# A decoder block with 32 streamed experts on one core: order of VectorE's mixing steps, of the router's products and table, of the third expert's first fetch, and of the last bias product

## Chip, core and metric

The kernel runs on one core of one Trainium2 chip, in float32. The time is the device time of the whole kernel in microseconds. Below, PE is TensorE, DVE is VectorE, ACT is ScalarE, POOL is GpSimd and SP is SyncE, whose queue issues nearly all loads.

## What is computed

```python
def reference(x, ...):                 # x: 1 x 256 x 1024, one layer
    u = rms_norm(h, norm1_g)
    proj = u @ w_in                    # 1024 x 4608
    y_conv = conformer_conv(proj[..., :c1], ...)          # ends in @ w_conv_out
    y_attn = moba_attention(q, k, v, ...) @ w_attn_out    # 8 heads of 64
    g = sigmoid(proj[..., c4:] + b_gates)
    mixed = g[..., :D] * y_conv + g[..., D:] * y_attn
    h = h + mixed @ w_out
    u2 = rms_norm(h, norm2_g)
    h = h + moe_ffn(u2, ...)           # 32 experts, the 4 best of each token

def moe_ffn(xf, ...):
    logits = xf @ w_router + b_router
    top_v, top_i = top_k(logits, 4); gates = softmax(top_v)
    # for each expert e, its tokens in rows:
    #   h = x @ w_up_gate[e] + b_up_gate[e]
    #   a = min(h[:, :F], 7); lin = clip(h[:, F:], -7, 7)
    #   y = (a * sigmoid(1.702 a) * (lin + 1)) @ w_down[e] + b_down[e]
    #   out[token] += y * gate
```

There are 256 tokens and 1024 features. An expert has 8 MiB of up and gate weights and 4 MiB of down weights, and every one of the 32 is used.

## The kernel before

The engines run hand-written instruction streams side by side and wait for each other through semaphores; nothing is scheduled by a compiler. On each engine the order is that of the code.

**Mixing stage.** Products of float32 weights are made of three products each: a high part times a high part, and each high part times the other's low part (`product3`, L1084). ACT writes high parts (`weights_high`, L537), DVE the low ones (`weights_low`, L728), in halves `b` of a weight group `i`: `ATT_W` is w_attn_out, `CONV_W` w_conv_out, `OUT_W` and `OUT_W + 1` the halves of w_out. PE makes four banks of attention products (uses `U_ATT + b` of the four shared banks), four banks of conv products (`U_CONV + b`), which go into the same banks, and then the products of w_out, with 512 columns each. Before it writes a bank it claims it: it waits until the last reader of that bank, four uses back, has freed it. DVE multiplies the attention banks with their gates (L862, the mixing products), and for each conv bank it makes a product and a sum (L877 and L881), which complete a quarter of `mixT` (`mix_ready`). ACT copies the quarter as a high part (`mix_hi`), and DVE makes its low part (`mix_low`, L869), for which PE's w_out products wait.

**Router.** PE turns the new h (`transpose_h`), DVE scales it to `u2T`, and `logits(m)` multiplies token tile m with the router's weights (L1061). Four `seed` products (L1275) put h into the four accumulator banks of the output. DVE finds the four best experts of each token; from these come tables in several steps that go back and forth between DVE and PE: positions of tokens (L1294 to L1298), number of tiles of 32 slots per expert (`exp_col[:, 0]`), keys that put experts with many tiles at turns in the order of experts (L1302, L1309), the experts at their turns (L1320 to L1322), ends (L1335), and last the rows that go to the integer table `cum` (L1339 to L1343). `cum` holds the first item of each turn, the expert and tile of each item, and the order of experts; its last write is signalled by `cum_ready` (L1002). Between these steps PE gathers the rows of the first tile (L1286), turns the gates (L1315, copied by ACT to `gates_t`), and makes the bias product of the first tile (`bias`, L1326).

**Experts.** Expert by expert in the order of the table, PE runs `tile` once per 32 slots: up products (L1365, 8 steps k, 32 matmuls that the trace counts as 64), scatter of the tile before (L1349), gather of the next, the bias product of the next tile (L1326), and down products (L1396). Each step's end is signalled: `up_quarter` after k = 1 (first expert only), `up_done[0]` after k = 3, `up_done[1]` after k = 7, `down_done`.

**Weights.** There are two buffers of each kind, even and odd. The parts of experts 0 and 1 are loaded by fixed number while the stages before still run, as their space in the buffers comes free: SP waits for PE's use of the scratch that lies there (`used(sp, i)`, `mix_ready`, `out_half`). Every later expert is fetched by its number, which SP reads from `cum` with a register load (`value_load`): `fetch` waits for `up_done` and `down_done` of the expert two turns earlier. The third expert's up weights go in quarters (`fetch_up_sooner`, L422), the first of them behind `up_quarter`.

## Time and profile before

| | |
|---|---|
| time, median of 3 runs | 1107.93 us (1107.56 to 1110.68) |
| profiled execution | 1109.64 us, its span 1107.9 us |
| granted TensorE clock, mean | 0.908 |
| PE, DVE, ACT busy | 918.5, 448.4, 252.4 us |
| loaded from HBM | 431.59 MB, 391 GB/s over the span |

The span is from the first to the last instruction in the trace. A busy share of an engine is an average over stages that have different limits. The granted clock is the share of full speed that the chip allows PE in a stretch: 1.00 is 2.4 GHz and 0.50 is 1.2 GHz. Times within the span are counted from its start.

### The profile page before, as it was taken

Reading aid. Unit: us, or ns where it says so; the run is one execution under the profiler, and the core shown is the slowest. Engines: PE = TensorE matmul, PEld = TensorE weight load, DVE = VectorE, ACT = ScalarE, POOL = GpSimd, SP = SyncE. Lnnn points to the kernel's source line nnn. Section 1 sums busy time; section 2 is a strip of 40 time slices with the busy share of each in tenths; the row PEclk is TensorE's granted clock in tenths of the full one; section 3 lists DMA queues with packets and bytes.
Section 4 is the critical chain, followed back from the end, with each engine's and each line's share of the span. In section 5 each row is a group of like instructions: output and inputs, shape, how many; then the busy total and the mean of one; then the engine's idle time right before and its main releaser. Section 6 shows DMA issues by size and latency. Waiting matters only on the chain.

```text
span 1107.9 us, 18786 instructions
## 1 busy us (share of the span) xinstructions
PE 918.5 (83%) x7003; PEld 425.0 (38%) x7004; DVE 448.4 (40%) x1106; ACT 252.4 (23%) x404; POOL 6.0 (1%) x29
## 2 busy tenths in 40 slices
PE   7999999998666669789976799986995965997666
PEld 6998888532111123233322233331331321332122
DVE  5899875442222223334432244442441422343222
ACT  4665573221111111212221011121220211122111
POOL 1000000000000000000000000000000000000000
PEclk9999899898788788889998899998997988998878
DMA  7664278999999999999999999999999999999996
GB/s 278 217 245 153 77 289 343 378 434 432 427 431 433 434 433 431 427 433 435 434 429 428 431 435 434 433 427 431 433 435 432 431 427 433 435 434 429 428 430 272
DMA packets 30647, 432.98 MB, mean 391 GB/s; under 512 B 2725, under 2 KB 3137, under 8 KB 16288
## 3 DMA queue, kind: packets, MB, share of 16 engines
q1 hardware_dynamic: 29640, 431.83, 92.1%
q10 hardware_dynamic: 984, 0.82, 0.2%
q8 instruction: 17, 0.28, 0.1%
q14 instruction: 6, 0.05, 0.0%
HBM read 431.59 MB, written 1.05 MB: 391 GB/s over the span
## 4 chain that ended last, share of the span: by engine, by line
PE 59%; DMA 28%; another core or an unknown queue 6%; DVE 4%; ACT 2%; issue 1%; SPq 0%; ACTq 0%; DVEq 0%
PE bank L1365 26%; DMA up_even<-in_w_up_gate 16%; PE bank L1396 10%; PE bank L1084 9%; DMA up_odd<-in_w_up_gate 8%; DMA down_even<-in_w_down 4%; PE bank L1349 3%; PE bank L1326 3%; PE bank L1286 3%; DVE up_odd L759 2%; DMA down_odd<-in_w_in 1%; DVE w_lo L728 1%; PE bank L1061 1%; PE bank L1379 1%
## 5 line engine op out<-in xcount | busy, mean ns | idle before, releaser
L1365 PE MATMUL bank<-up_even,reg_r 128*32 128x512 f32 x1472 | 204.6, 714 | 77.0 <-DMA up_even<-in_w_up_gate 77.0
L1365 PE MATMUL bank<-up_odd,reg_r 128*32 128x512 f32 x1408 | 183.9, 677 | 74.9 <-DMA up_odd<-in_w_up_gate 74.9
L1044 DVE SCALAR_TENSOR_TENSOR ys<-bank,gslot,ys 64x512 fp32r<-64x512 f32 x90 | 67.4, 749 | 228.7 <-ACT ys L683 227.2
L1365 PEld LDWEIGHTS bank<-up_even,reg_r 128*32 128x32 f32 x1472 | 53.4, 128 | 224.1 <-issue 139.2
L683 ACT ACTIVATE ys<-bank,gslot 64x512 fp32r<-64x512 f32 x90 | 61.5, 683 | 315.3 <-PE bank L1396 314.1
L1365 PEld LDWEIGHTS bank<-up_odd,reg_r 128*32 128x32 f32 x1408 | 48.7, 123 | 207.4 <-issue 123.7
L677 ACT ACTIVATE reg_m<-reg_m 128x256 f32<-128x256 f32 x45 | 18.9, 420 | 429.5 <-DVE reg_m L1023 429.5
L1396 PE MATMUL bank<-down_odd,reg_r 128*32 128x512 f32 x704 | 81.8, 606 | 11.1 <-DMA down_odd<-in_w_down 11.1
L1023 DVE TENSOR_SCALAR reg_m<-bank 128x256 f32<-128x256 f32 x45 | 19.1, 425 | 172.8 <-PE bank L1365 172.8
L1396 PE MATMUL bank<-down_even,reg_r 128*32 128x512 f32 x736 | 83.7, 595 | 4.8 <-DMA down_even<-in_w_down 4.8
L677 ACT ACT_TABLE_LOAD x45 | 57.7, 1283 | 6.9 <-issue 6.1
L1349 PE MATMUL bank<-ys,hotT 128*128 128x512 f32 x184 | 55.3, 421 | 1.8 <-DVE ys L1044 1.8
L1084 PE MATMUL bank<-u_hi,w_hi 128*128 128x256 f32 x176 | 52.3, 297 | 0.9 <-issue 0.9
L1326 PE MATMUL bank<-bup,sel 128*128 128x512 f32 x92 | 52.7, 655 | 0.0
L1084 PE MATMUL bank<-u_lo,w_hi 128*128 128x256 f32 x176 | 50.7, 288 | 0.0
L1084 PE MATMUL bank<-u_hi,w_lo 128*128 128x256 f32 x176 | 50.7, 288 | 0.0
L1286 PE MATMUL bank<-reg_h,reg_r 128*32 128x256 f32 x736 | 49.3, 385 | 0.7 <-DVE reg_r L910 0.7
L920 DVE TENSOR_SCALAR sel<-quarter_of,pick 128x128 f32<-128x128 f32 x46 | 13.1, 284 | 88.8 <-PE bank L1365 88.8
L759 DVE SCALAR_TENSOR_TENSOR up_odd<-up_odd,reg_m 128x256 f32<-128x256 f32 x120 | 48.6, 482 | 0.0
L1349 PEld LDWEIGHTS bank<-ys,hotT 128*128 128x128 f32 x184 | 30.9, 188 | 45.8 <-issue 38.6
L910 DVE TENSOR_SCALAR reg_r<-iota,pos,st 128x32 f32 (+1 forms) x92 | 23.3, 298 | 61.2 <-issue 61.2
L1396 PEld LDWEIGHTS bank<-down_odd,reg_r 128*32 128x32 f32 x704 | 21.0, 111 | 69.3 <-issue 49.2
(250 smaller groups left out, 1077.4 us busy)
## 6 DMA issues: line engine op xcount, KB each, us to landing
up_odd<-in_w_up_gate SPq DMA_DIRECT2D x30, 4096.0 KB, 47.1
up_even<-in_w_up_gate SPq DMA_DIRECT2D x28, 4096.0 KB, 39.7
down_even<-in_w_down SPq DMA_DIRECT2D x15, 4096.0 KB, 42.6
down_odd<-in_w_down SPq DMA_DIRECT2D x14, 4096.0 KB, 46.8
up_even<-in_w_up_gate SPq DMA_DIRECT2D x7, 2048.0 KB, 11.9
down_even<-in_w_in SPq DMA_DIRECT2D x6, 2048.0 KB, 8.6
up_odd<-in_w_up_gate SPq DMA_DIRECT2D x4, 2048.0 KB, 11.9
down_odd<-in_w_down SPq DMA_DIRECT2D x8, 1024.0 KB, 32.2
```

Source lines behind the costliest of these rows:

```text
L677: nc.scalar.activation(ACT_B, ACT_A, ACT.Sigmoid, scale=ALPHA).then_inc(sigm_ready, 1)
L683: nc.scalar.activation(ys[0:64, half, :], YB[r, :], ACT.Identity, scale=gslot[r, :]).then_inc(y_high, 1)
L759: ins = nc.vector.scalar_tensor_tensor(cv[:, c, :], tap, dwT[:, c, w:w + 1], cv[:, c, :], ALU.mult, ALU.add)
L910: nc.vector.tensor_scalar(hot[:, m, :], slot, pos[:, m, e], st[:, 6 + m:7 + m], ALU.is_equal, ALU.mult).then_inc(hot_built, 1)
L1023: nc.vector.tensor_scalar(ACT_A, UP[:, 0:256], LIMIT, None, ALU.min).then_inc(clip_ready, 1)
L1044: nc.vector.scalar_tensor_tensor(ys[64:P, half, :], YB[r, :], gslot[0:64, :], ys[0:64, half, :].bitcast(F32), ALU.mult, ALU.subtract).then ...
L1084: ins = mm(o, lhs(a, k), rhs(b, k), start=(k == 0 and i == 0), stop=(k == n - 1 and i == 2))
L1286: ins = mm(o[q * SLOTS:(q + 1) * SLOTS, 0:256], hot[:, m, :], hx[:, m, 256 * q:256 * q + 256], start=(m == 0), stop=(m == MT - 1))
L1326: mm(UP[:], sel[:], bup[:], start=True, stop=False, skip_group_check=True)
L1349: ins = mm(acc[2 * m + half][:], hotT[:, m, :], ys[:, half, :], start=False, stop=False, skip_group_check=True)
L1365: ins = mm(UP[q * SLOTS:(q + 1) * SLOTS, :], XT[:, k, :], up_columns(a, k, q), start=False, stop=(k == KD - 1), skip_group_check=True)
L1396: ins = mm(YB[row:row + SLOTS, :], actT[:, r, :], down[a][:, r, half * 512:(half + 1) * 512], start=(r < 2), stop=(r >= KD - 2), skip_grou ...
```

## The change

It has four parts.

1. In DVE's mixing stage the four mixing products come ahead of the low part of w_conv_out's second half; the low part of w_out's second half goes behind the third sum.
2. In the router the halves of `logits(0)` stand around the second tile's transposes, the fourth seed stands behind the product L1302, the first bias product ahead of the turn products, the product that gives the order with the turn products, and the gate products are cut in two. They have their own bank part (`GT`) and semaphores.
3. DVE writes the number of tiles of the first expert (`T_LEAD`) and the order of experts to `cum` as soon as it has them, with a semaphore for each. SP reads the third expert's number behind these, and waits for `cum_ready` only behind its fetch.
4. In the tile of the last expert the next bias product goes behind the down products.

```diff
         UP, ROWS, GA, YB = bank[0:4]
+        GT = ROWS[2 * E:4 * E, T:2 * T]
         def up_columns(a, k, q):
...
             load_down(1, 0, 1)
-            sp.wait_ge(cum_ready, 1)
             def expert_of(t):
...
                 down(a, e, items)
-            fetch(2, 0, fetch_down, fetch_up_sooner)
+            sp.wait_ge(lead_ready, 1)
+            lead = sp.value_load(cum[0:1, T_LEAD:T_LEAD + 1], min_val=1, max_val=ITEMS - 1)
+            sp.wait_ge(order_ready, 1)
+            third = expert_of(2)
+            fetch_up_sooner(0, third, lead)
+            fetch_down(0, third, lead)
+            sp.wait_ge(cum_ready, 1)
             fetch(3, 1, fetch_down)
...
             ins.then_inc(expg, 1)
-            full(act, U_GT)
-            nc.scalar.activation(gT[:], bank[U_GT % 4][0:2 * E, 0:T], ACT.Identity).then_inc(bank_free[U_GT % 4], 1)
+            act.wait_ge(gt_full, 1)
+            nc.scalar.activation(gT[:], GT, ACT.Identity).then_inc(gt_copied, 1)
             act.wait_ge(cum_ready, 1)
...
                 nc.vector.tensor_tensor(conv_half(cv_r[1], b), conv_half(cv, b), conv_half(cv_r[0], b).bitcast(F32), ALU.subtract).then_inc(cv_lo, 1)
-            weights_low(CONV_W, 1)
             for b in range(4):
                 u = U_ATT + b
                 full(dve, u)
                 freed(dve, LAST_USE[GROUPS - 1])
                 nc.vector.tensor_tensor(mixT[:, 2 * b:2 * b + 2, :], bank[u % 4][:].rearrange("p (a b) -> p a b", a=2),
                                         gates[:, 8 + 2 * b:10 + 2 * b, :], ALU.mult).then_inc(bank_free[u % 4], 1)
-            for b in range(2):
-                weights_low(OUT_W, b)
-            def mix_low(b):
-                dve.wait_ge(mix_hi, b + 1)
-                m = slice(2 * b, 2 * b + 2)
-                nc.vector.tensor_tensor(u_r[1][:, m, :], mixT[:, m, :], u_r[0][:, m, :].bitcast(F32), ALU.subtract).then_inc(mix_lo, 1)
-            for b in range(4):
+            weights_low(CONV_W, 1)
+            weights_low(OUT_W, 0)
+            def mix_add(b):
                 u = U_CONV + b
...
                 nc.vector.tensor_tensor(mixT[:, 2 * b:2 * b + 2, :], mixT[:, 2 * b:2 * b + 2, :], prod, ALU.add).then_inc(mix_ready, 1)
-                if b >= 1:
-                    mix_low(b - 1)
+            def mix_low(b):
+                dve.wait_ge(mix_hi, b + 1)
+                m = slice(2 * b, 2 * b + 2)
+                nc.vector.tensor_tensor(u_r[1][:, m, :], mixT[:, m, :], u_r[0][:, m, :].bitcast(F32), ALU.subtract).then_inc(mix_lo, 1)
+            mix_add(0)
+            mix_add(1)
+            mix_low(0)
+            mix_add(2)
+            mix_low(1)
+            weights_low(OUT_W, 1)
+            mix_add(3)
+            mix_low(2)
             mix_low(3)
...
             rows_scale(0)
+            nc.vector.tensor_copy(cum[0:1, T_LEAD:T_LEAD + 1], exp_col[0:1, 0:1]).then_inc(lead_ready, 1)
             full(dve, U_TURN)
-            nc.vector.tensor_copy(by_turn[:], bank[U_TURN % 4][0:E, 0:2]).then_inc(bank_free[U_TURN % 4], 1)
+            nc.vector.tensor_copy(by_turn[:], bank[U_TURN % 4][0:E, 0:2]).then_inc(turn_copied, 1)
+            nc.vector.tensor_copy(cum[0:1, T_ORDER:T_ORDER + E], bank[U_TURN % 4][0:1, 64:64 + E]).then_inc(order_ready, 1)
             full(dve, U_ENDS)
...
             done(nc.vector.tensor_copy(cum[0:1, T_EXPERT:T_EXPERT + ITEMS], ib[0:1, 64:64 + ITEMS]))
-            done(nc.vector.tensor_copy(cum[0:1, T_ORDER:T_ORDER + E], ib[0:1, 192:192 + E]))
             step(nc.vector.tensor_tensor(trow, iota[0:1, 0:ITEMS], ib[0:1, 128:128 + ITEMS], ALU.subtract))
...
                     ins.then_inc(bank_full[u % 4], 1)
-            def logits(m):
-                for b in range(2):
-                    freed(pe, U_U2T + 2 * m + b)
-                return product(bank[U_LOG % 4][:, m * E:(m + 1) * E], lambda k: u2T[:, k, m * P:(m + 1) * P], lambda k: wr[:, k, :], KD)
+            def logits(m, b):
+                freed(pe, U_U2T + 2 * m + b)
+                for k in range(4 * b, 4 * b + 4):
+                    ins = mm(bank[U_LOG % 4][:, m * E:(m + 1) * E], u2T[:, k, m * P:(m + 1) * P], wr[:, k, :],
+                             start=(k == 0), stop=(k == KD - 1))
+                return ins
             split(OUT_W + 1, 0)
...
             claim(U_LOG)
-            logits(0)
+            logits(0, 0)
             transpose_h(1)
+            logits(0, 1)
+            logits(1, 0)
+            logits(1, 1).then_inc(bank_full[U_LOG % 4], 1)
             def seed(j):
                 return mm(acc[j][:], ident[:], hx[:, j // 2, j % 2 * 512:(j % 2 + 1) * 512], start=True, stop=False, skip_group_check=True)
-            seed(0)
-            logits(1).then_inc(bank_full[U_LOG % 4], 1)
-            seed(1)
-            seed(2)
-            seed(3)
+            for j in range(3):
+                seed(j)
             def gather(o):
...
             mm(bank[U_WIDE % 4][0:E, 0:1], tri[0:E, 0:E], wide[:], start=True, stop=True).then_inc(bank_full[U_WIDE % 4], 1)
+            seed(3)
             pe.wait_ge(hot_built, MT)
...
             mm(bank[U_KEYS % 4][0:E, 0:E], key[:, 3:4].to_broadcast([E, E]), ident[0:E, 0:E], start=True, stop=True).then_inc(bank_full[U_KEYS % 4], 1)
-            pe.wait_ge(gate_ready, 1)
-            claim(U_GT)
-            for m in range(MT):
-                for half in range(2):
-                    ins = mm(bank[U_GT % 4][half * E:(half + 1) * E, m * P:(m + 1) * P], gate[:, m, :], ident[:], start=True, stop=True)
-            ins.then_inc(bank_full[U_GT % 4], 1)
+            def bias(n):
+                pe.wait_ge(sel_ready, n + 1)
+                mm(UP[:], sel[:], bup[:], start=True, stop=False, skip_group_check=True)
+            freed(pe, U_LOG)
+            pe.wait_ge(bup_in, 64)
+            bias(0)
             freed(pe, U_KEYS)
             claim(U_TURN)
             o = bank[U_TURN % 4]
             mm(o[0:E, 0:1], at_turn[:, 0:E], exp_col[:, 0:1], start=True, stop=True)
             mm(o[0:E, 1:2], at_turn[:, 0:E], exp_col[:, 2:3], start=True, stop=False)
-            mm(o[0:E, 1:2], at_turn[:, 1:E + 1], exp_col[:, 1:2], start=False, stop=True).then_inc(bank_full[U_TURN % 4], 1)
-            def bias(n):
-                pe.wait_ge(sel_ready, n + 1)
-                mm(UP[:], sel[:], bup[:], start=True, stop=False, skip_group_check=True)
-            freed(pe, U_GT)
-            pe.wait_ge(bup_in, 64)
-            bias(0)
-            freed(pe, U_TURN)
+            mm(o[0:E, 1:2], at_turn[:, 1:E + 1], exp_col[:, 1:2], start=False, stop=True)
+            mm(o[0:1, 64:64 + E], exp_col[:, 1:2], at_turn[:, 0:E], start=True, stop=True).then_inc(bank_full[U_TURN % 4], 1)
+            def gates_turned(m):
+                for half in range(2):
+                    ins = mm(GT[half * E:(half + 1) * E, m * P:(m + 1) * P], gate[:, m, :], ident[:], start=True, stop=True)
+                return ins
+            pe.wait_ge(gate_ready, 1)
+            gates_turned(0)
+            pe.wait_ge(turn_copied, 1)
             claim(U_ENDS)
             tiles, jump = by_turn[:, 0:1], by_turn[:, 1:2]
             mm(bank[U_ENDS % 4][0:E, 0:1], tri[0:E, 0:E], tiles, start=True, stop=False)
             mm(bank[U_ENDS % 4][0:E, 0:1], ident[0:E, 0:E], tiles, start=False, stop=True).then_inc(bank_full[U_ENDS % 4], 1)
-            claim(U_ITEMS)
+            gates_turned(1).then_inc(gt_full, 1)
+            pe.wait_ge(order_ready, 1)
             ib = bank[U_ITEMS % 4]
             mm(ib[0:1, 0:E + 1], tiles, tri[0:E, 0:E + 1], start=True, stop=True)
-            mm(ib[0:1, 192:192 + E], exp_col[:, 1:2], at_turn[:, 0:E], start=True, stop=True)
             freed(pe, U_ENDS)
...
                 pe.wait_ge(hot_built, MT * n + 2 * MT)
+                if first:
+                    pe.wait_ge(gt_copied, 1)
                 gather(ROWS)
-                pe.wait_ge(clip_ready, n + 1)
-                pe.wait_ge(lin_ready, n + 1)
-                bias(n + 1)
+                def next_bias():
+                    pe.wait_ge(clip_ready, n + 1)
+                    pe.wait_ge(lin_ready, n + 1)
+                    bias(n + 1)
+                if not last:
+                    next_bias()
                 pe.wait_ge(actT_ready, n + 1)
...
                 ins.then_inc(down_done[DOWNS - 1], 1)
+                if last:
+                    next_bias()
             def tiles_of(e, a, pair, last=False):
```

DVE's rows in the mixing stage, from conv's own low halves (cv_lo) on, before. w_lo_50 with w_hi_52 is w_conv_out's second half, w_lo_51 is w_out's first group:

```order
L854 TENSOR_TENSOR cv_lo<-up_odd,cv_hi 128x512 [waits cv_hi,cT_ready] x2
L728 TENSOR_TENSOR w_lo_50<-down_even,w_hi_52 128x4x512 [waits w_hi_ready]
L862 TENSOR_TENSOR down_odd<-bank,up_odd 128x512 [waits bank_free3,bank_full0]
L862 TENSOR_TENSOR down_odd<-bank,up_odd 128x512 [waits bank_free3,bank_full1]
L862 TENSOR_TENSOR down_odd<-bank,up_odd 128x512 [waits bank_free3,bank_full2]
L862 TENSOR_TENSOR down_odd<-bank,up_odd 128x512 [waits bank_free3,bank_full3]
L728 TENSOR_TENSOR w_lo_51<-down_even,w_hi_53 128x2048 [waits w_hi_ready] x2
L877 TENSOR_TENSOR reg_r<-bank,up_odd 128x512 [waits bank_full0]
L881 TENSOR_TENSOR down_odd<-down_odd,reg_r 128x512 [waits bank_free0]
```

And in the changed kernel:

```order
L861 TENSOR_TENSOR cv_lo<-up_odd,cv_hi 128x512 [waits cv_hi,cT_ready] x2
L866 TENSOR_TENSOR down_odd<-bank,up_odd 128x512 [waits bank_free3,bank_full0]
L866 TENSOR_TENSOR down_odd<-bank,up_odd 128x512 [waits bank_free3,bank_full1]
L866 TENSOR_TENSOR down_odd<-bank,up_odd 128x512 [waits bank_free3,bank_full2]
L866 TENSOR_TENSOR down_odd<-bank,up_odd 128x512 [waits bank_free3,bank_full3]
L735 TENSOR_TENSOR w_lo_50<-down_even,w_hi_52 128x4x512 [waits w_hi_ready]
L735 TENSOR_TENSOR w_lo_51<-down_even,w_hi_53 128x2048 [waits w_hi_ready]
L876 TENSOR_TENSOR reg_r<-bank,up_odd 128x512 [waits bank_full0]
```

The four products that read the banks moved ahead of one low part, and of the two low parts of w_out's first group only one still stands before the first sum.

PE's rows in the router, from the key product (L1309) to the first of the last table products, before:

```order
L1309 MATMUL bank<-ident,reg_m 32x32 [waits bank_free1,bank_free3]
L1315 MATMUL bank<-ident,gate 32x128 [waits bank_free0,gate_ready]
L1315 MATMUL bank<-ident,gate 32x128 x3
L1320 MATMUL bank<-reg_m 32x1 [waits bank_free3,bank_free1]
L1321 MATMUL bank<-reg_m 32x1
L1322 MATMUL bank<-reg_m 32x1
L1326 MATMUL bank<-bup,sel 128x512 [waits sel_ready,bup_in,bank_free0]
L1335 MATMUL bank<-reg_m 32x1 [waits bank_free1,bank_free3]
L1336 MATMUL bank<-reg_m,ident 32x1
L1339 MATMUL bank<-reg_m 1x33 [waits bank_free3]
L1340 MATMUL bank<-reg_m 1x32
L1342 MATMUL bank<-reg_r,reg_m 1x64 [waits bank_free1]
L1343 MATMUL bank<-reg_r,reg_m 1x64
```

And in the changed kernel, where L1324 is the key product, L1328 the bias, L1337 to L1340 the turn products with that of the order, and L1344 the gates:

```order
L1324 MATMUL bank<-ident,reg_m 32x32 [waits bank_free1,bank_free3]
L1328 MATMUL bank<-bup,sel 128x512 [waits sel_ready,bup_in,bank_free0]
L1337 MATMUL bank<-reg_m 32x1 [waits bank_free3,bank_free1]
L1338 MATMUL bank<-reg_m 32x1
L1339 MATMUL bank<-reg_m 32x1
L1340 MATMUL bank<-reg_m 1x32
L1344 MATMUL bank<-ident,gate 32x128 [waits gate_ready]
L1344 MATMUL bank<-ident,gate 32x128
L1353 MATMUL bank<-reg_m 32x1 [waits bank_free1,turn_copied]
L1354 MATMUL bank<-reg_m,ident 32x1
L1344 MATMUL bank<-ident,gate 32x128 x2
L1358 MATMUL bank<-reg_m 1x33 [waits order_ready]
L1360 MATMUL bank<-reg_r,reg_m 1x64 [waits bank_free1]
```

The bias product moved from behind the turn products to before them, the gate products from before them to behind them in two pieces, and the product of 1x32 for the order now ends the turn products.

SP's rows from the last load by a fixed number to the first fetch, before:

```order
L354 DMA down_odd<-in_w_down 128x2048 [waits bank_full0]
L409 TENSOR_LOAD cum [waits cum_ready]
L409 ISA x2
L406 TENSOR_LOAD cum
L406 ISA x2
L422 ISA [waits up_quarter]
L422 DMA up_even<-in_w_up_gate 128x4096
```

And in the changed kernel:

```order
L356 DMA down_odd<-in_w_down 128x2048 [waits bank_full0]
L448 TENSOR_LOAD cum [waits lead_ready]
L448 ISA x2
L407 TENSOR_LOAD cum [waits order_ready]
L407 ISA x2
L423 ISA [waits up_quarter]
L423 DMA up_even<-in_w_up_gate 128x4096
```

The register loads wait for the two new semaphores in place of the last table's.

## Rows read from the trace of the kernel before

**Rows 1.** The page's slices: GB/s moved in each of 40.
```profile
GB/s 278 217 245 153 77 289 343 378 434 432 427 431 433 434 433 431 427 433 435 434 429 428 431 435 434 433 427 431 433 435 432 431 427 433 435 434 429 428 430 272
```

**Rows 2.** Windows, the stream: window, length, busy PE, PEld, DVE, ACT, POOL (count), PEclk, DMA share, GB/s.
```profile
221.25:1095.00 873.75, 706.01 (x5526) 240.98 (x5522) 279.26 (x799) 135.44 (x177) 0.00 (x0) 0.90 1.00 432
```

**Rows 3.** Windows where the DMA engines stood still or started.
```profile
172.00:176.00 4.00, 4.00 (x35) 4.00 (x34) 2.31 (x4) 1.02 (x2) 0.00 (x0) 1.00 0.00 0
...
217.50:217.75 0.25, 0.25 (x4) 0.00 (x0) 0.00 (x0) 0.00 (x0) 0.00 (x0) 0.50 0.35 98
...
219.75:220.00 0.25, 0.25 (x8) 0.00 (x0) 0.00 (x0) 0.00 (x0) 0.00 (x0) 0.50 0.00 0
...
221.25:221.50 0.25, 0.25 (x8) 0.09 (x4) 0.10 (x1) 0.00 (x0) 0.00 (x0) 1.00 1.38 590
```

**Rows 4.** Timeline of SP's queue: start, us, queue, line, transfer, count.
```profile
176.05 0.81 SPq L354 DMA_DIRECT2D down_even<-in_w_down  x2
...
219.15 0.36 SPq L422 DMA_DIRECT2D up_even<-in_w_up_gate  x1
...
506.78 0.34 SPq L415 DMA_DIRECT2D up_even<-in_w_up_gate  x1
```

**Rows 5.** Timeline of PE between attention and conv: start, us, ..., [idle before <-releaser].
```profile
159.96 0.28 PE L1084 MATMUL bank<-ao_hi,w_lo 128*128 128x256 f32 x1
...
162.78 0.35 PE L1084 MATMUL bank<-cv_hi,w_hi 128*128 128x256 f32 x1 [2.54 <-DVE w_lo L728]
```

**Rows 6.** Windows at the low clock.
```profile
165.00:166.00 1.00, 1.00 (x6) 1.00 (x6) 1.00 (x1) 0.00 (x0) 0.00 (x0) 0.50 1.05 406
...
211.00:211.25 0.25, 0.25 (x6) 0.03 (x2) 0.22 (x2) 0.00 (x0) 0.00 (x0) 0.50 0.46 197
```

**Rows 7.** Timeline of DVE in the mixing stage.
```profile
157.45 1.29 DVE L854 TENSOR_TENSOR cv_lo<-up_odd,cv_hi 128x512 fp32r<-128x512 f32 x2 [0.17 <-ACT cv_hi L636]
...
159.79 2.29 DVE L728 TENSOR_TENSOR w_lo<-down_even,w_hi 128x2048 fp32r<-128x2048 f32 x1 [1.04 <-ACT w_hi L537]
...
162.00 2.48 DVE L862 TENSOR_TENSOR down_odd<-bank,up_odd 128x512 f32<-128x512 f32 x4
...
164.39 4.48 DVE L728 TENSOR_TENSOR w_lo<-down_even,w_hi 128x2048 fp32r<-128x2048 f32 x2
...
173.18 0.69 DVE L877 TENSOR_TENSOR reg_r<-bank,up_odd 128x512 f32<-128x512 f32 x1 [0.86 <-PE bank L1084]
...
176.06 0.69 DVE L877 TENSOR_TENSOR reg_r<-bank,up_odd 128x512 f32<-128x512 f32 x1 [0.86 <-PE bank L1084]
```

**Rows 8.** The chain that ended last: start, us, what.
```profile
162.78 33.68 PE bank L1084 x186
...
200.43 0.52 PE bank L1252 x4
...
204.36 2.66 PE bank L1275 x6
...
212.12 2.01 PE bank L1326 x2
...
413.52 3.67 another core or an unknown queue
...
430.79 6.91 PE bank L1365 x64
```

**Rows 9.** Timeline of PE and DVE at the router's end.
```profile
215.28 9.97 PE L1365 MATMUL bank<-up_even,reg_r 128*32 128x512 f32 x64
...
215.95 0.18 DVE L1002 TENSOR_SCALAR cum<-reg_r 1x64 int32<-1x64 f32 x1
```

**Rows 10.** Timeline of DVE and PE in the last tile.
```profile
1094.58 0.65 DVE L1032 STREAM_TRANSPOSE reg_r<-reg_m 128x256 f32<-128x256 f32 x1
...
1095.41 1.12 PE L1326 MATMUL bank<-bup,sel 128*128 128x512 f32 x2
...
1096.46 1.06 PE L1396 MATMUL bank<-down_odd,reg_r 128*32 128x512 f32 x8
```

5 lines of the change are left out of this document (3 added, 2 removed).

## Prediction

> **What bounds the kernel now.** I read the page's slices first: from the ninth to the last but one they move 427 to 435 GB/s, whatever PE (TensorE) does [rows 1]. Taken together, from 221.25 to 1095 us the share of the DMA engines is 1.00 at 432 GB/s, while PE is busy for 706 of the 874 us [rows 2]. Thirty experts of 12 MiB are fetched in that time, 377 MB, and at 432 GB/s these are 874 us: the stream of expert weights is the whole of it, and nothing that PE does inside counts unless it lets the stream run dry. So the end is the moment at which the stream starts, plus 874 us, plus a tail behind the last weight. Next I asked what sets the start. The loads for experts 0 and 1 run out shortly before 217.5, the engines stand still at 219.75, and the flow is back at 221.25 [rows 3]. What brings it back is SyncE's first fetch for the third expert, issued at 219.15 [rows 4], 3.0 us behind the last table write at 215.95+0.18 [rows 9]: two register loads, 1.5 us each. So two things are worth time: when the loads ahead of it end, and when this fetch may go.
>
> Those loads are 16 MiB, issued from 176.05 on [rows 4], when PE is through with its conv products. The engines had been idle from 172 to 176 [rows 3] and are busy from then on. Last I read why PE is late there. It stood 2.54 us before its first conv product at 162.78 [rows 5], and behind that wait its clock was 0.50 (the 1.2 GHz level): 6 matmuls in the microsecond from 165 [rows 6], against 35 in four at 1.00 (2.4 GHz) [rows 3].
>
> **The mixing stage.** PE ends its attention products at 159.96+0.28 = 160.24 [rows 5], and its conv product may claim a bank once VectorE (DVE) has read it in the first mixing product L862. That product stood behind the low part L728 at 159.79, which waited 1.04 us for ScalarE's high part, and ran at 162.00 [rows 7]. Put ahead, it starts when conv's own low halves end, 157.45+1.29 = 158.74, and frees the bank at 159.5, before PE asks. PE goes on at 160.24 with no wait. A bank of conv products takes 2.88 us at the full clock (DVE's last two sums were released by PE at 173.18 and 176.06 [rows 7]), so four end at 160.24+11.52 = 171.76 and not 176.05: 4.3 us, 2.54 of it the wait and 1.75 the low clock after it. If the clock fell here all the same, the 1.75 would be lost; I take them, since nothing is left that lets PE stand.
>
> What is late next? DVE in its new order, by its own rows [rows 7]: four products, 0.62 each, to 161.3 (the last bank is full at 160.24); two low parts of 2.24 to 165.8; two sums, two steps of 0.69 and their gaps each, to 168.8; the first low part of mix to 169.4; the third sum to 170.9 and its low part to 171.5; the low part of w_out's second half to 173.8; the fourth sum to 175.3; the last low parts to 176.6. PE takes 0.227 us for a product of 512 columns (186 pieces from 162.78 take 33.68 us [rows 8], and the 90 of them behind 176.05 take 20.4). It wants the second mix low part at 173.2 (there at 171.5), the second half of w_out and the third low part at 177.2 (173.8 and 175.9), the fourth at 178.6 (176.6). The smallest reserve is 1.3 us. The next weights start on ScalarE behind the fourth sum and are through DVE near 180.5, wanted at 182.7. So all that follows moves by 4.3.
>
> **The router.** Only half of logits(0) stands now before the second token tile's transposes, so they start 0.83 earlier than 200.43 [rows 8], and four products of the logits run while DVE scales, where a seed ran. The logits end near 203.05 and not at 204.36 [rows 8]: 1.3 us. Three seeds still follow, 2.66 us [rows 8], which end with DVE's selection as before. The fourth, some 0.9, fills a wait before the first gather and delays it by 0.1. Expert 0's bias product goes from behind the turn products to before them; it took 2.01 us of the chain at the low clock [rows 8], and takes 1.12 at the full one [rows 10] beside DVE's turn chain. The order's matmul and cast now come with the turn products (0.2), the gate products are split around the next wait and add nothing outside it, and the copy of gates_t is wanted only by tile 0's later gather. By this count tile 0 gains 1.1 us more; at the low clock all through, 0.35. In sum 4.3+1.3+1.1 = 6.7: its first product goes from 215.28 [rows 9] to 208.6.
>
> **The fetch and the stream.** The loads ahead are released by PE and move by 4.3, from about 217.35 to 213.05. The first fetch no longer waits for the last table. Lead and order are written near 207, two register loads of 1.5 give 209.8, and PE's first quarter (2 of 8 steps of a tile of 6.91 [rows 8] at the full clock, 1.7) is done at 210.4: issue at 210.6. From the issue to flow on idle engines took 2.1 us (219.15 to 221.25), so it could flow at 212.7, just before the engines are free at 213.05. The hole closes, and the stream starts 221.25-213.05 = 8.2 us earlier. Does the middle keep that? The thinnest reserve that I find is at 506.78 [rows 4], behind an expert of nine tiles: the 120 MiB issued from 219.15 until then flow until 512.5, 5.7 us behind that issue, of which 2 go for its start. But PE entered this expert at 430.79 just behind a wait for weights at 413.52 [rows 8], so its issues move with the stream and the reserve stays.
>
> **The tail.** In the last tile DVE's transposed activations are ready at 1094.58+0.65 = 1095.23, but PE runs the bias product of a tile that never comes from 1095.41, and the down products only at 1096.46 [rows 10]. Behind them it lies in PE's wait for ys. Gain 1.05 us.
>
> **Sum.** 8.2+1.05 = 9.25 us. The profiled execution took 1109.64 for its span of 1107.9, 1.71 above the median of the runs shown; 1109.64-9.25-1.71 = 1098.7 for the median.
>
> **The clock, weighed.** It was 0.50 at 211.00 [rows 6] and at 219.75, and back at 1.00 at 221.25 [rows 3], after a stretch in which PE waited little but had mostly narrow products. In the new order a seed and a bias product of full width lie there, but from the turn products to tile 0 there are still 2.3 us of narrow ones. The Trainium skill, "TensorE: Matmul & The Clock Gate", section "What's actually happening", says that the slow state is the default, that activity releases it, and that the watching runs freely of the kernel, so that the point of change varies. By that rule the new order may meet the slow clock in one execution and not in the next; no run here shows that yet.
>
> **Rivals.**
> - *The clock falls before tile 0's first quarter is done.* For it: its state at 211.00 and the narrow products that remain. Against: two dense products put into just this stretch. Tile 0 starts at 209.4, the quarter takes 3.4, the issue is at 213.0 and the flow at 215.1: 6.15+1.05 = 7.2 us, 1100.7. The skill's "DMA: Bandwidth & Descriptors", section "Specifications", has some 0.6 us to the first byte on this kind of queue; by that figure this rival would come to 1099.2. The trace has no such start on idle engines but the one of 2.1 us at 219.15.
> - *The mixing stage gives nothing*, because DVE becomes its bound or PE meets another wait and the low clock. For it: DVE is busy without a break from 158.8 to 173.8, with a reserve of 1.3. Then the loads end at 217.35 as before, the fetch (tile 0 at 212.9, issue at 214.9) comes in time, and the hole closes: 3.9+1.05 = 5.0 us, 1103.0.
> - *The stream runs dry behind an expert of many tiles.* If PE's place there did not move, the gain would be cut to a reserve of about 4 plus 1.05: 1102.9. Against it speaks the wait at 413.52.
> - *Slower.* The stream is 874 us, so 1.1% less bandwidth costs the whole 9.25, and from 1.5% less (under 426 GB/s) the kernel is slower by over 0.3%. Loads and fetch meeting without a pause could be served worse; at 425 GB/s it gives 1113. Against: no slice of the stream is under 427 [rows 1].
>
> **How the numbers follow.** Forecast 0.5; low clock 0.27; no gain in mixing 0.13; dry stream 0.05; lower bandwidth 0.05. The time is that of the first, 1098.7. Reserves and median may each be off by a microsecond, so the low end is 1096.8; the high end takes in the second and third cases, 1103.0. A measurement of this kernel tells about 0.3%, 3.3 us, from no change. The first four cases are beyond it, less a share for several at once: faster 0.91, within 0.3% 0.05, slower 0.04.
>
> **What the new profile would show.** PE goes from its attention to its conv products with no wait and at clock 1.00, and these end near 171.8; the idle of the DMA engines from 172 to 176 shrinks to about 1 us; tile 0 starts at 208 to 209.5; the third expert's first fetch is issued at 210.5 to 213, held by PE's quarter and by no table; the DMA share has no hole, or one under 2 us, between 212 and 216; down products follow the gather in the last tile. The prediction is wrong if conv ends later than 174, if the clock is at 0.50 from the router on, or if the share falls under 1.00 anywhere behind 220.

## The result, and the profile after

The changed kernel takes 1102.07 us in the median of 5 runs (1101.84 to 1103.49), against 1107.93 (1107.20 to 1110.68) for the kernel before in the same session: a ratio of 0.9944, with a 95% interval of 0.9928 to 0.9959. That is 5.9 us less. Forecast were 9.2 us and 1098.7. The direction was right and the range held the time, but the gain is over a third smaller than the sum said.

The page of the profiled execution (1103.49 us, its span 1101.7; the execution of before took 1109.64 and its span 1107.9) has this row of slices, which answers to [rows 1]:

```profile
GB/s 285 211 248 153 77 254 402 420 430 432 432 431 433 431 432 432 435 429 432 433 431 432 432 432 431 432 432 431 433 432 431 433 432 431 432 435 431 432 431 283
```

The stream still runs at 429 to 435 GB/s; it starts earlier. The seventh and eighth slice moved 343 and 378 GB/s before, and now 402 and 420. The timeline of PE where attention ends and conv begins, against [rows 5]:

```profile
161.50 0.28 PE L1096 MATMUL bank<-ao_hi,w_lo 128*128 128x256 f32 x1
161.62 0.28 PE L1096 MATMUL bank<-cv_hi,w_hi 128*128 128x256 f32 x1
```

The wait of 2.54 us is gone. DVE in its new order, against [rows 7]:

```profile
160.19 2.48 DVE L866 TENSOR_TENSOR down_odd<-bank,up_odd 128x512 f32<-128x512 f32 x4
162.58 4.48 DVE L735 TENSOR_TENSOR w_lo<-down_even,w_hi 128x2048 fp32r<-128x2048 f32 x2
...
175.31 0.69 DVE L880 TENSOR_TENSOR down_odd<-down_odd,reg_r 128x512 f32<-128x512 f32 x1
175.92 1.47 DVE L885 TENSOR_TENSOR u_lo<-down_odd,u_hi 128x512 fp32r<-128x512 f32 x2
```

SP's queue, against [rows 4]: the loads behind the conv products, and the third expert's first fetch.

```profile
173.33 0.81 SPq L356 DMA_DIRECT2D down_even<-in_w_down  x2
...
211.91 5.97 SPq L423 DMA_DIRECT2D up_even<-in_w_up_gate  x4
```

PE at the router's end, against [rows 9]:

```profile
204.72 1.13 PE L1292 MATMUL bank<-reg_h,ident 128*128 128x512 f32 x2
205.78 1.07 PE L1300 MATMUL bank<-reg_h,reg_r 128*32 128x256 f32 x16
...
206.96 1.12 PE L1328 MATMUL bank<-bup,sel 128*128 128x512 f32 x2
...
209.77 1.50 PE L1383 MATMUL bank<-up_even,reg_r 128*32 128x512 f32 x12
```

And windows (length, busy PE, PEld, DVE, ACT, POOL, PEclk, DMA share, GB/s), against [rows 3] and [rows 6]:

```profile
132.00:133.00 1.00, 1.00 (x4) 0.55 (x2) 0.31 (x2) 0.66 (x2) 0.00 (x0) 0.50 1.05 422
156.00:226.00 70.00, 69.67 (x499) 51.08 (x501) 44.18 (x93) 25.21 (x39) 0.77 (x2) 1.00 0.98 396
...
173.00:174.00 1.00, 1.00 (x7) 0.87 (x6) 1.00 (x1) 0.00 (x0) 0.00 (x0) 1.00 0.55 229
174.00:175.00 1.00, 1.00 (x6) 0.80 (x6) 1.00 (x2) 0.00 (x0) 0.00 (x0) 1.00 0.81 139
175.00:176.00 1.00, 1.00 (x6) 0.84 (x5) 0.96 (x3) 0.00 (x0) 0.00 (x0) 1.00 0.88 360
...
212.00:224.00 12.00, 12.00 (x112) 4.76 (x108) 4.81 (x16) 1.70 (x2) 0.00 (x0) 1.00 1.02 414
172.00:300.00 128.00, 110.95 (x781) 53.43 (x784) 49.54 (x136) 26.13 (x41) 0.77 (x2) 0.93 1.00 423
```

The clock is 1.00 from 156 to 226 us, where before it was 0.50 twice. But it is 0.50 at 132 in this execution and was 1.00 there before, and so everything up to the mixing stage stands 1.54 us later (161.50 against 159.96). That has nothing to do with the change, which begins behind it. The same two windows of the kernel before:

```profile
212.00:224.00 12.00, 11.90 (x73) 3.48 (x75) 2.54 (x14) 1.28 (x1) 0.00 (x0) 0.62 0.82 316
172.00:300.00 128.00, 112.23 (x780) 55.13 (x778) 49.15 (x137) 26.61 (x42) 0.77 (x2) 0.91 0.95 401
```

From 172 to 300 us the new kernel moved 22 GB/s x 128 us = 2.8 MB more. At 432 GB/s that is 6.5 us of the stream. (With the window shifted by the 1.54 us, from 173.54 to 301.54, it is 423 GB/s as well.)

The last attention product starts between 159.49 and 161.50 us in these executions, whatever the kernel, so I compare by stages that start at a mark of their own. All are read from timelines of PE and SP: (a) from the start of PE's last attention product to SP's issue at the end of the conv products; (b) from there to tile 0's first up product; (c) from there to the last 32 up products; (d) from these to the transposes behind them; (e) from these to the end of the span.

| execution profiled | (a) | (b) | (c) | (d) | (e) | a to c |
|---|---|---|---|---|---|---|
| before | 16.09 | 39.23 | 872.18 | 6.30 | 14.14 | 927.50 |
| before, again (e0) | 16.09 | 37.90 | 871.34 | 6.20 | 14.17 | 925.33 |
| part 4 alone (e2) | 16.11 | 39.41 | 872.33 | 6.26 | 12.93 | 927.85 |
| parts 2 and 3 alone (e3) | 14.59 | 36.41 | 873.15 | 5.98 | 14.18 | 924.15 |
| before, wait filled (e6) | 14.59 | 37.87 | 871.84 | 6.24 | 14.18 | 924.30 |
| part 1 alone (e1) | 11.84 | 37.86 | 871.93 | 6.30 | 14.18 | 921.63 |
| after | 11.83 | 36.44 | 872.72 | 6.29 | 12.92 | 920.99 |
| after, again (e7) | 11.83 | 36.42 | 872.85 | 7.57 | 12.97 | 921.10 |
| after, fetch late (e5) | 11.84 | 36.44 | 873.16 | 7.57 | 12.99 | 921.44 |
| after, more ahead (e8) | 11.84 | 36.42 | 872.61 | 7.51 | 12.97 | 920.87 |
| after, tail filled (e11) | 11.83 | 36.40 | 873.23 | 4.60 | 14.19 | 921.46 |
| more ahead, tail filled (e12) | 11.84 | 36.40 | 871.85 | 4.60 | 14.15 | 920.09 |

Stage (a) lies at 16.1, 14.6 or 11.8 in twelve profiles and (b) near 39.3, 37.9 or 36.4. Executions of like clock agree in stages (a) and (b) within 0.2 us, where the times of whole kernels can't tell a microsecond. Stage (c) is less sharp: before and e2 run the same program at the same clock up to the last up products, and a to c differs by 0.35 us. Differences in a to c below some 0.4 us are not told apart from nothing.

### The profile page after: what moved, and what is told of

It is laid out like the page before. It is cut to its first block, busy times and chain, and to the rows that moved or that the text cites. A ratio compares the mean times of both kernels' runs of the same rounds, so it can differ in the third digit from the quotient of the medians.

```text
span 1101.7 us, 18785 instructions
## 1 busy us (share of the span) xinstructions
PE 913.7 (83%) x7003; PEld 423.5 (38%) x7004; DVE 448.2 (41%) x1107; ACT 252.5 (23%) x404; POOL 6.0 (1%) x29
## 3 DMA queue, kind: packets, MB, share of 16 engines
HBM read 431.59 MB, written 1.05 MB: 393 GB/s over the span
## 4 chain that ended last, share of the span: by engine, by line
PE 59%; DMA 29%; another core or an unknown queue 6%; DVE 4%; ACT 1%; issue 0%; SPq 0%; ACTq 0%; DVEq 0%
PE bank L1383 26%; DMA up_even<-in_w_up_gate 16%; PE bank L1096 10%; PE bank L1420 10%; DMA up_odd<-in_w_up_gate 8%; DMA down_even<-in_w_down 4%; PE bank L1367 3%; PE bank L1328 3%; PE bank L1300 3%; DVE up_odd L766 2%; DMA down_even<-in_w_in 1%; DVE w_lo L735 1%; PE bank L1397 1%; PE bank L1395 1%
## 5 line engine op out<-in xcount | busy, mean ns | idle before, releaser
L1383 PE MATMUL bank<-up_even,reg_r 128*32 128x512 f32 x1472 | 200.6, 702 | 77.3 <-DMA up_even<-in_w_up_gate 77.3
L1383 PE MATMUL bank<-up_odd,reg_r 128*32 128x512 f32 x1408 | 186.4, 685 | 76.5 <-DMA up_odd<-in_w_up_gate 76.5
L1328 PE MATMUL bank<-bup,sel 128*128 128x512 f32 x92 | 51.8, 645 | 0.0
L1420 PEld LDWEIGHTS bank<-down_even,reg_r 128*32 128x32 f32 x736 | 22.9, 109 | 63.3 <-issue 63.3
```

Of the source, the lines that this page charges most:

```text
L1328: mm(UP[:], sel[:], bup[:], start=True, stop=False, skip_group_check=True)
L1383: ins = mm(UP[q * SLOTS:(q + 1) * SLOTS, :], XT[:, k, :], up_columns(a, k, q), start=False, stop=(k == KD - 1), skip_group_check=True)
L1420: ins = mm(YB[row:row + SLOTS, :], actT[:, r, :], down[a][:, r, half * 512:(half + 1) * 512], start=(r < 2), stop=(r >= KD - 2), skip_grou ...
```

## Experiments

Each ratio is to the kernel before on the same chip, with its 95% interval. Where a gain is given behind a ratio, it is worked out from the ratio.

### The kernel before once more, and the parts alone

**The kernel before, unchanged.** No edit.

> The kernel before, unchanged, to see what one execution may differ from another by. Theory A (the changed kernel's gain is a sum of moves of the weight stream, and the forecast of 9.25 us missed by a stream hole that was really 2.7 us wide and not 3.9, and by a slow-clock stretch at 131 us that fell into its profiled execution and cost 1.5) expects a median within 0.15% of 1107.9 and a trace in which the slow-clock stretches lie at other places than before, each moving what is behind it by 1 to 2 us. Rival B (the clock falls at fixed places of the program) expects the slow clock again at 112, 163, 211 us and nowhere else ahead of 230.

It took 1108.16 us (ratio 0.9997, 0.9982 to 1.0012). PE's timeline and windows (columns as above):

```profile
163.52 0.36 PE L1084 MATMUL bank<-cv_hi,w_hi 128*128 128x256 f32 x1 [2.55 <-DVE w_lo L728]
```

```profile
165.00:166.00 1.00, 1.00 (x6) 1.00 (x6) 1.00 (x2) 0.00 (x0) 0.00 (x0) 0.50 1.07 416
...
211.00:212.00 1.00, 0.92 (x14) 0.49 (x10) 0.83 (x4) 0.00 (x0) 0.00 (x0) 1.00 0.92 393
212.00:224.00 12.00, 11.44 (x108) 5.28 (x110) 5.16 (x22) 2.08 (x3) 0.00 (x0) 1.00 1.01 398
```

The wait and the low clock behind it are there again, but the low clock at the router's end is not. With it go 1.33 us of stage (b) and 2.2 us up to the last up products, and from 212 to 224 us 398 GB/s are moved in place of 316. The hole on which 3.9 us of the forecast stood is, for the most part, a property of executions that meet this low clock, as the one did that I had read. Neither expectation of the places holds whole: the low clock came at 112 and 163 us as before, and at 211 it did not.

**Part 1 alone**, DVE's new order in the mixing stage (shortened):

```diff
-            weights_low(CONV_W, 1)
             for b in range(4):
                 ... # mixing products
-            for b in range(2):
-                weights_low(OUT_W, b)
+            weights_low(CONV_W, 1)
+            weights_low(OUT_W, 0)
```

> The kernel before with the new order of VectorE's mixing steps alone. Theory A: PE enters its conv products with no wait and at the full clock, the conv products end 4.3 us earlier relative to the attention products, and the whole stream moves by that, the hole ahead of the third expert stays as it is: 1103.6 us. Rival C (the mixing order only moves the wait to a later place): 1106 to 1108. Rival D (mixing is all of the gain, the rest of the change nothing): 1102.

1104.63 us, ratio 0.9963 (0.9948 to 0.9977): 4.1 us less. Stage (a) is 4.25 shorter than in both executions of the kernel before, and of these 3.70 arrive at the last up products (925.33 to 921.63). This part is most of the change.

**Parts 2 and 3 alone**, the router's order and the early fetch, as in the diff of the change.

> The changed kernel without the new mixing order and without the late bias of the last expert: the router's order and the early fetch alone. Theory A: the hole of the stream closes, worth 2.7 us at the third expert, 1105.2 us; the loads for experts 0 and 1 end where they did. Rival D: 1107.9, as before.

1107.31 us, ratio 0.9988 (0.9973 to 1.0003): 1.3 us less, and no change is not excluded. PE's timeline, and a window behind its wait:

```profile
162.31 0.35 PE L1092 MATMUL bank<-cv_hi,w_hi 128*128 128x256 f32 x1 [2.54 <-DVE w_lo L735]
```

```profile
165.00:166.00 1.00, 1.00 (x11) 1.00 (x10) 1.00 (x1) 0.00 (x0) 0.00 (x0) 1.00 1.05 395
```

The same wait, 2.54 us, and here the clock stays at 1.00 behind it: 11 matmuls in the microsecond in place of 6. So the low clock of the mixing stage isn't a sure consequence of the wait. It costs 1.50 us (16.09 against 14.59) in executions in which it comes. In stage (b) the new router saves 1.46 at the full clock (37.87 in e6, 36.41 here).

**Part 4 alone**, the last bias product:

```diff
+                if not last:
+                    next_bias()
                 pe.wait_ge(actT_ready, n + 1)
...
+                if last:
+                    next_bias()
```

> The kernel before with only the bias product of the last expert's tile behind its down products. Theory A: the down products follow the gather and the end comes 1.05 us earlier, 1106.9 us. Rival (the bias product hid a wait for ACT, DVE or the last weights): no change, 1107.9.

1108.48 us, ratio 0.9996 (0.9981 to 1.0010). The timing can't show 1.2 us; stage (e) does: 12.93 against 14.14 and 14.17. The low clock at the router's end came in this execution too (39.41 in stage (b)).

### The early fetch, and the wait filled

**The changed kernel again.** No edit.

> The changed kernel once more, beside the three below. Theory A2 (as A, with what the first runs showed: the slow-clock stretches at 163 and 211 us of the kernel before do not come in every execution; without them its waits are worth 2.54 us in mixing, 0.7 at the stream's hole and 1.2 in the tail, with them 4.3, 2.7 and 1.2) expects 1102 us and fewer slow stretches than before, since its PE neither waits at the conv products nor has long narrow stretches in the router. Rival B2 (the gain does not hang on the clock) expects the same gain, but the same trace marks relative to before in every execution.

1102.96 us, ratio 0.9942 (0.9923 to 0.9961).

**The changed kernel with the fetch behind the last table:**

```diff
-            sp.wait_ge(lead_ready, 1)
-            lead = sp.value_load(cum[0:1, T_LEAD:T_LEAD + 1], ...)
-            sp.wait_ge(order_ready, 1)
-            third = expert_of(2)
-            fetch_up_sooner(0, third, lead)
-            fetch_down(0, third, lead)
             sp.wait_ge(cum_ready, 1)
+            fetch(2, 0, fetch_down, fetch_up_sooner)
```

> The changed kernel, but SyncE reads the third expert's number only behind the last table write, as before. Theory A2: the fetch is issued about 1.5 us later (213.5 for 211.9), the loads for experts 0 and 1 run out at 214.3, so the hole is 1 us wide at most: 0.5 to 1 us slower than the changed kernel, 1102.6 to 1103. Rival F (the early fetch is what closed the hole of 3.9 us, and is worth as much): 1105 or more.

1102.97 us, ratio 0.9947 (0.9928 to 0.9966), beside 1102.96 for the changed kernel on the same chip. SP's first fetch is issued 2.32 us behind tile 0's start (210.40 and 208.08) and not 2.15 (209.96 and 207.81). Once PE is early, two register loads behind the last table end nearly when PE's first quarter does, and the new semaphores have little left to win: the fetch goes 0.2 us earlier, and the 0.34 us up to the last up products (921.44 and 921.10) are within what two executions of one program differ by.

**The kernel before with PE's wait filled** by 18 products whose result nobody reads:

```diff
+            pe.wait_ge(cv_lo, 1)
+            for j in range(18):
+                mm(bank[4][:, 0:256], cv_r[0][:, 0, 0:P], cv_r[0][:, 0, :], start=True, stop=True)
```

> The kernel before with 18 products of no use put into PE's wait ahead of the conv products, written to a bank that nobody reads at that time; what it computes stays the same. They take 2.2 of the 2.54 us, so the wait itself stays and only the clock can gain. Theory A2: no slow stretch at 163 in any execution, 1.75 us less where there was one: the median 0.9 to 1.75 lower than before, 1106.5 to 1107.3, and the conv products end 11.5 us behind the first. Rival B2: the products only lengthen PE's queue, 1108 to 1109.

1107.01 us, ratio 0.9984 (0.9971 to 0.9996). PE's timeline and a window:

```profile
160.00 2.32 PE L1238 MATMUL bank<-cv_hi 128*128 128x256 f32 x18
162.70 0.35 PE L1084 MATMUL bank<-cv_hi,w_hi 128*128 128x256 f32 x1 [0.38 <-issue]
```

```profile
165.00:166.00 1.00, 1.00 (x11) 1.00 (x10) 1.00 (x1) 0.00 (x0) 0.00 (x0) 1.00 1.05 403
```

The conv products begin as late as before, at the full clock, and stage (a) is 1.50 shorter. In a single profile this could be the luck of e3. The times of all executions speak for the filling, by 0.4 to 3.2 us (the interval just leaves 1 out); that the clock is the reason is argued from the one profile. e6 and e3 also answer what the router and the fetch bring when the clock is alike: 1.46 us in stage (b), and nothing that can be told at the last up products (924.30 and 924.15).

### What else could start the stream earlier, and its end

**More fetched ahead.** The changed kernel with one piece of 1 MiB of expert 1's up weights issued before its turn, to use the thin place at 173 to 175 us. The second piece of the load that is split for this stays where it was:

```diff
+            freed(sp, U_ATT + 3)
+            load_up_row(1, 1, 1)
...
-            load_up(1, 0, 1)
+            load_up_row(1, 0, 1)
```

> The changed kernel with one more step in the same direction: 1 MiB of expert 1's up weights is loaded as soon as the four mixing products have read the gates that lie in its place, near 163 us, and not behind the fourth sum at 176. The trace of the changed kernel has the DMA engines idle or half idle for 1.6 us from 173.4 on. If the stream is bounded by when the loads ahead of it end, filling that hole moves it by 1.0 to 1.6 us: 1100.5 to 1101. If the third expert's fetch now bounds it, or the clock decides, no change: 1102.

1101.84 us, ratio 0.9935 (0.9916 to 0.9953), the lowest ratio of all, but not told apart from the changed kernel's 0.9942 and 0.9944. Up to the last up products it stands 0.23 us before e7, which is not told apart either. Windows of e7 and then of e8:

```profile
172.00:173.00 1.00, 1.00 (x6) 0.83 (x5) 1.00 (x2) 0.00 (x0) 0.00 (x0) 1.00 0.70 106
212.00:224.00 12.00, 12.00 (x108) 4.62 (x104) 4.91 (x14) 1.96 (x4) 0.00 (x0) 1.00 1.03 410
```

```profile
172.00:173.00 1.00, 1.00 (x6) 0.83 (x5) 1.00 (x2) 0.00 (x0) 0.00 (x0) 1.00 1.00 418
212.00:224.00 12.00, 12.00 (x108) 4.60 (x104) 4.86 (x14) 1.86 (x4) 0.00 (x0) 1.00 0.98 398
```

The thin place was filled, and the stream is thinner by 12 GB/s where the third expert's fetch takes over (issued 38.56 us behind the conv products in e8, 38.57 in e7). That fits the case in which this fetch now bounds the start.

**The end.** In e7 PE reached its last up products early, and lost 1.3 us of it in stage (d): 7.57 us in place of 6.30. The timeline and windows of e7:

```profile
1071.02 6.30 PE L1383 MATMUL bank<-up_odd,reg_r 128*32 128x512 f32 x32 [6.06 <-DMA up_odd<-in_w_up_gate]
...
1080.66 6.60 PE L1383 MATMUL bank<-up_odd,reg_r 128*32 128x512 f32 x32 [3.33 <-DMA up_odd<-in_w_up_gate]
```

```profile
1081.00:1083.00 2.00, 2.00 (x12) 0.39 (x8) 0.00 (x0) 0.00 (x0) 0.00 (x0) 0.50 1.03 430
1083.00:1085.00 2.00, 2.00 (x16) 0.47 (x12) 0.00 (x0) 0.00 (x0) 0.00 (x0) 0.50 1.01 422
```

PE waits for the last weights, then multiplies at 0.50 of the clock. So I filled these two waits in the changed kernel:

```diff
             def tile(n, a, pair, first=False, last=False):
+                if last:
+                    pe.wait_ge(hotT_ready, n + 1)
                 for k in range(KD):
                     if k % UPK == 0:
+                        for j in range((22 if k == 0 else 22) if last else 0):
+                            mm(GA[:], gT[:, 0:P], bdown[:, 0:512], start=True, stop=True, skip_group_check=True)
```

> The changed kernel with 22 products of 512 columns, whose result nobody reads, in TensorE's wait before each half of the last expert's up products (22 x 0.227 = 5.0 us; these waits are 5.9 and 3.3 to 4.5 us in the profiles so far). In those profiles the last 32 up products take 5.3 to 6.6 us, because the clock is 0.50 behind the waits; at the full clock they would take 3.5. Theory (what an earlier start of the stream wins is partly given back here, since the clock falls behind the wait for the last weights): the clock stays at 1.00, the last up products take 3.5 to 3.7, the transposes behind them start 1.8 to 3.0 earlier counted from the first of these products, and with the down products then held by the last weights, which land until some 2 us behind the transposes, the kernel takes 1100.0 to 1101.5. Rival one (only the stream decides the end, the down products wait for the last weights anyway): no change, 1102 to 1103. Rival two (the clock falls all the same): the products of the filling take 0.45 each, 10 us a wait, and the kernel takes 1105 to 1108.

1126.36 us, ratio 1.0162 (1.0148 to 1.0176). And the same with the early piece of e8 (the expectation says two pieces; as in e8, one goes early):

> The same filling, in the changed kernel with two pieces of 1 MiB more fetched ahead (one behind attention's low halves, one behind the conv products). The pieces moved 0.3 MB more until 300 us in the profile of that kernel, 0.7 us of the stream, and its profiled execution was 0.2 us shorter than the changed kernel's. Theory: the two gains add, 1099.5 to 1101. Rival one: 1101.5 to 1102.5. Rival two: 1104 to 1108.

1126.82 us, ratio 1.0167 (1.0150 to 1.0183). Both fillings were mis-sized, by neither rival's mechanism. PE's timeline and windows of the first:

```profile
1065.65 19.15 PE L1384 MATMUL bank<-reg_m,gates_t 64*128 64x512 f32 x44
1084.73 3.64 PE L1387 MATMUL bank<-up_odd,reg_r 128*32 128x512 f32 x32
```

```profile
1066.00:1068.00 2.00, 2.00 (x6) 0.85 (x5) 1.27 (x2) 1.96 (x3) 0.00 (x0) 1.00 0.95 410
...
1085.00:1087.00 2.00, 2.00 (x24) 0.62 (x20) 0.00 (x0) 0.00 (x0) 0.00 (x0) 1.00 1.01 422
```

The operands of these products are plain f32, not the rounded kind of the weights' products, and one takes 0.87 us and not 0.227. I put it down to the kind of operand, which no run here changes alone; the router's three seeds of h, plain f32 and of 512 columns too, took 2.66 us [rows 8], 0.89 each. But the clock stayed at 1.00, and the 32 up products took 3.64. So the filling was cut to 6 a wait:

```diff
-                        for j in range((22 if k == 0 else 22) if last else 0):
+                        for j in range(6 if last else 0):
```

> The filling of the last expert's two waits with 6 products each in place of 22. In the trace of the run with 22 one of them takes 0.87 us (22 in 19.15, both operands are plain f32), so that filling overran the waits by 13 us; 6 take 5.2 us, in waits of some 6 us. In that trace the clock was 1.00 all through and the last 32 up products took 3.64 us. Theory: the same here with no overrun; from the start of these products to the transposes behind them 4.6 us or less (6.3 in the changed kernel's profile, 7.6 in its second look); the time 1100.0 to 1101.5. Rival one (the last weights decide): 1102 to 1103. Rival two (a lone filling that ends 0.8 us before the weights land doesn't hold the clock): the last up products take over 5 us, and the time is 1102 to 1103 as well; the clock tells it from rival one.

1101.79 us, ratio 0.9942 (0.9928 to 0.9955). PE's timeline:

```profile
1082.81 3.64 PE L1387 MATMUL bank<-up_odd,reg_r 128*32 128x512 f32 x32 [1.63 <-DMA up_odd<-in_w_up_gate]
...
1092.71 1.07 PE L1424 MATMUL bank<-down_odd,reg_r 128*32 128x512 f32 x8 [0.99 <-DMA down_odd<-in_w_down]
```

Stage (d) is down to 4.60, and a new wait stands in stage (e), which grows from 12.97 to 14.19: the last quarter of the down products now waits 0.99 us for its weights. The theory and rival one are each right in part: the clock is held, and the last weights then decide. The time lies between their two ranges.

The same with the early piece of e8:

> The same 6 products for each wait in the kernel with the two pieces of 1 MiB fetched ahead. Theory: 1099.5 to 1101, at or below the kernel above by up to 0.7. Rival: pieces and filling don't add, and it stands with the kernel above within 0.3 us or over it.

1101.14 us, ratio 0.9943 (0.9929 to 0.9956). Its profiled execution has the shortest span of all, 1098.6, with a to c at 920.09. The medians of e11, e8 and e12 are 1101.79, 1101.84 and 1101.14, their ratios all within the interval of the changed kernel's. So the gain of up to 0.7 us that e12 was to show over e11 (0.65 by the medians, nothing by the ratios) is not shown. I have no version that measurably beats the changed kernel.

## Why the prediction was right in sign and too large

**The bound: right.** The end moved with the start of the stream, and the stream itself stayed 431 to 432 GB/s. Stage (c) varies by 1.9 us over the kernels of the table.

**Mixing, 4.3 us = 2.54 wait + 1.75 low clock: right in the profiled pair, 4.26 (16.09 to 11.83).** At the same clock (e6 and e3 against e1) the wait is worth 2.75; the low clock is worth 1.50, and e3 shows that the kernel before doesn't always pay it. DVE kept its places, no PE wait took the old one's place, and w_out's products were not held up. The DMA engines' idle from 172 to 176 is now a thin place: 229, 139 and 360 GB/s in the three microseconds from 173, 1.3 us short of 432.

**Router, 2.4 us for tile 0: met in the pair (39.23 to 36.44, 2.79), for the wrong reason.** At the full clock it is 1.46. The rest, 1.33, is the low clock, which e2 met as well and e0, e1 and e6 did not. Of this the forecast had 0.89 in its sum (the bias product, 2.01 at the low clock and 1.12 at the full one), as if its new place had won it.

**The hole, 3.9 us: the step that failed.** "The hole closes, and the stream starts 221.25-213.05 = 8.2 us earlier." The marks were right: with the 1.54 us taken off, tile 0 came at 208.23 (forecast 208.6) and the first fetch at 210.37 (210.6), and behind 212 us there is no hole. What was wrong is the price, in two ways, and the reason for the late fetch.
- The hole was not empty. From 212 to 224 us the kernel before moved 316 GB/s, 3.79 MB; 432 would have been 5.18. The gap is 1.39 MB or 3.2 us, and 0.5 us of it (414 GB/s) is left after. That makes 2.7, not 3.9. Over all, a to c fell by 6.51 and not by 8.2, just the 6.5 us of bytes counted above.
- Most of it came only with the low clock. With the clock at 1.00 at 211 us (e0) the same window moved 398 GB/s, a gap of 0.9 us. At the full clock the router and the early fetch together bring 0.53 us (e1 to e7), and between e6 and e3 0.15.
- The fetch was late for another reason. The prediction lays the 3.0 us between the last table write and the fetch at 219.15 to two register loads of 1.5 us. But SP also waited for PE's first quarter there, 1.4 us by its waits from 216 to 220:

```profile
SPq L409 <- DVE cum L1002: 11.4, 1, 11.4
SPq L422 <- PE bank L1365: 1.4, 1, 1.4
```

In e0 no such wait stands before the fetch, and it goes 1.61 us behind the last table write:

```profile
215.32 0.18 DVE L1002 TENSOR_SCALAR cum<-reg_r 1x64 int32<-1x64 f32 x1
...
217.11 5.68 SPq L422 DMA_DIRECT2D up_even<-in_w_up_gate  x4
```

In e1, e6 and e5 it is 1.60 or 1.61 as well. So two register loads take at most 1.6 us together, 0.8 each, and in the execution of before the fetch hung on tile 0's first quarter at the low clock (3.87 us from tile 0's start to the fetch, 2.42 in e0, 2.15 in e7). From the end of the conv products to the fetch it took 43.10 us in before and 43.28 in e2, 40.32 in each of e0, e1 and e6, and 38.55 to 38.58 in after, e7, e3 and e8. The low clock is worth 2.8 us or more of this, and the new router and semaphores together 1.75, of which the semaphores are 0.2 (e5, 38.76).

The 2.1 us that the prediction reads from the issue to the flow are wrong, too. The engines stood still at 219.75 and moved at full rate half a microsecond later, then hardly until 221.25:

```profile
220.00:220.50 0.50, 0.50 (x8) 0.10 (x4) 0.00 (x0) 0.00 (x0) 0.00 (x0) 0.50 2.16 492
220.50:221.00 0.50, 0.50 (x8) 0.10 (x4) 0.16 (x1) 0.00 (x0) 0.00 (x0) 0.50 0.11 33
```

So the first bytes came 1 us behind the issue, as they did at 177.0 behind the issue at 176.05, a second start on idle engines that the prediction says the trace hasn't. What held the flow from 220.5 to 221.25 stays open.

**The tail, 1.05 us: right, measured 1.22** (14.14 to 12.92).

**The end, not in the forecast.** In e7, e5 and e8 the products behind PE's last waits ran at the low clock for their whole length, and 1.3 us of an earlier stream were given back there. In the profiled execution of after the low clock covered only a part of them (5.34 us in place of 6.60), and stage (d) took 6.29 as in before.

**The median.** From before to after the stages a to e give 7.74 us, less 1.54 for the low clock at 132 us: 6.2, the difference of the spans. From e0 to e7 they give 4.06 (4.23 up to the last up products, 1.37 lost in stage (d), 1.20 won in stage (e)). The measured 5.9 lies between. So the forecast added up the prices of an execution in which the kernel before met the low clock twice, and took them for every execution's. It named the right places, and the range held the time because it was wide enough for this.

**The rivals.** The low clock before tile 0's first quarter did not come in any profile with the new router. It was in the profile of before that it held the fetch. The mixing stage gave what it should. The stream didn't run dry, and the bandwidth didn't fall. None of the rivals was the one that counted: that the low clock of the kernel before comes and goes by itself.

What stays open: how often the kernel before meets each stretch of low clock. Of four profiles with the wait unfilled (before, e0, e2, e3) three met the one behind it; of five with the old router two met the other (before and e2, not e0, e1 and e6). Which of them lies behind each of the times without a trace can't be told.

## What to carry to other kernels

Price a stretch of low clock only after a second look at the unchanged kernel: here the wait was there in each of four profiles, the slow products behind it in three. Price a hole in a transfer stream by the bytes that are missing from it, not by the time between its edges. When a stream sets the time, an earlier fetch is worth only what it takes from the gap ahead of it: here the fetch went 1.75 us earlier, the gap was 0.9 us, and at most 0.5 arrived. And where a transfer waits for two things, read from the queue's own waits which of them ended last before giving the time to either.

## What the runs showed of the hardware

- The same program meets the low clock at one place in one execution and not in the next: at 211 us in the first profile of the kernel before, not in the second, with the same instructions before it. The wait of 2.54 us was followed by 0.50 in e0 and by 1.00 in e3. The Trainium skill, "TensorE: Matmul & The Clock Gate", section "What's actually happening", says that the point of change varies since the watching runs freely of the kernel; these traces agree, and the stretches differ in whether they come at all.
- With products in the waits whose result nobody reads, the clock stayed at 1.00: in the mixing stage (e6, one profile, and e3 shows the same without them) and at the end, in four profiles (e9 to e12), even where an idle rest of 0.6 to 1.6 us was left. 32 of the last up products then took 3.64 us each time, and 4.9 to 6.6 us in every profile without the filling.
- The spread of the kernel before is 1105.4 to 1111.7 us over the 31 runs of one session, that of the changed one 1101.3 to 1103.5 over 11. Part 1 alone spreads over 3.5 us in 8 runs (1103.55 to 1107.05), parts 2 and 3 alone over 6.6 in 11 (1105.42 to 1111.97). So the kernels without the wait are the steadier ones; that the low clock behind it is the reason is not shown.
- The first bytes of a load on idle DMA engines came about 1 us behind SP's issue: between 220.1 and 220.2 us for 219.15, at 177.0 for 176.05.
- Two register loads and the steps between them took SP 1.6 us from the table write to the issue of the fetch (e0, e1, e6, e5).
